# Experts' loop turned by three weight pieces, with an adding indirect transfer per block in place of stores and gathers

## The reference, cut to what matters

```
logits = h @ router_w + router_b            # 512 x 32
top, ids = top_k(logits, 4); gate = softmax(top)
for each token t and each of its 4 experts e:
    up   = h[t] @ w1[e] + b1[e]             # 1024 -> 2 x 1024, a gate part and a linear part
    hid  = silu-like(min(gatepart, 7)) * (clip(linear, -7, 7) + 1)
    y[t] += gate[t, e] * (hid @ w2[e] + b2[e])
x = x + mod * y                             # then a last RMS norm is the output
```

## Time and profile before

| | us |
|---|---|
| median of 3 runs | 3776.75 (3775.6 to 3782.47) |
| the profiled execution | 3776.74 |
| its span, first to last instruction | 3774.8 |
| mean granted TensorE clock | 0.923 of 2.4 GHz |
| busy in the span: TensorE, VectorE, ScalarE, GpSimd | 3347.7, 2305.7, 1548.4, 117.1 |
| experts' loop, first weight matmul to last | 2488.2 to 3705.9 |
| combining, its first DMA to the last addition to the residual | 3717.3 to 3758.2 |

### The profile page before, as it was taken

The page is one execution under the profiler, slowest core; times in us unless marked ns, Lnnn a source line. Parts: engine busy times, 40 slices in busy tenths (PEclk is TensorE's granted clock), DMA queues, the critical chain, the costliest instruction groups (busy, mean ns, idle before and its releaser), DMA issues. The chain is left out here.

```text
span 3774.8 us, 47052 instructions
## 1 busy us (share of the span) xinstructions
PE 3347.7 (89%) x16502; PEld 2588.1 (69%) x16503; DVE 2305.7 (61%) x2926; ACT 1548.4 (41%) x1933; POOL 117.1 (3%) x113
## 2 busy tenths in 40 slices
PE   7887998999968878899987878879999999999996
PEld 5655886884446567788756655667777777777774
DVE  4375665347422454455444474478888888888885
ACT  1262332010033621100123153357777777777772
POOL 0000000000000000000000000000000000000001
PEclk8888999999979987799988989879999999999996
DMA  5401222232102000122273101279999999999995
GB/s 160 154 24 45 89 100 80 99 89 89 67 27 64 1 1 1 50 100 92 89 290 120 56 9 34 77 313 399 363 357 359 361 352 359 364 355 360 359 346 216
DMA packets 182773, 648.58 MB, mean 172 GB/s; under 512 B 14033, under 2 KB 95825, under 8 KB 126210
## 3 DMA queue, kind: packets, MB, share of 16 engines
q1 hardware_dynamic: 165474, 600.56, 43.6%
q0 software_dynamic: 7056, 25.69, 1.8%
q10 hardware_dynamic: 10128, 20.76, 1.4%
HBM read 612.83 MB, written 36.75 MB: 172 GB/s over the span
## 5 line engine op out<-in xcount | busy, mean ns | idle before, releaser
L488 DVE TENSOR_TENSOR experts_rest<-experts_weights,experts_leading 128x2048 fp32r<-128x2048 f32 x384 | 875.3, 2286 | 109.7 <-ACT experts_leading L2990 109.7
L2990 ACT CAST experts_leading<-experts_weights 128x2048 fp32r<-128x2048 f32 x384 | 716.9, 1907 | 50.7 <-ACT experts_y L2982 22.2
L494 PE MATMUL psum<-experts_leading,experts_xT_leading 128*128 128x512 f32 x1024 | 410.9, 401 | 51.5 <-DVE experts_rest L488 51.5
L496 PE MATMUL psum<-experts_leading,experts_xT_rest 128*128 128x512 f32 x1024 | 406.2, 397 | 0.0
L495 PE MATMUL psum<-experts_rest,experts_xT_leading 128*128 128x512 f32 x1024 | 405.6, 396 | 0.0
L494 PEld LDWEIGHTS psum<-experts_leading,experts_xT_leading 128*128 128x128 f32 x1024 | 194.7, 190 | 107.4 <-DVE experts_rest L488 65.3
L496 PEld LDWEIGHTS psum<-experts_leading,experts_xT_rest 128*128 128x128 f32 x1024 | 194.6, 190 | 46.8
L495 PEld LDWEIGHTS psum<-experts_rest,experts_xT_leading 128*128 128x128 f32 x1024 | 194.6, 190 | 43.8
L494 PE MATMUL psum<-experts_leading,experts_hidden_leading 128*128 128x512 f32 x512 | 210.3, 411 | 0.0
L496 PE MATMUL psum<-experts_leading,experts_hidden_rest 128*128 128x512 f32 x512 | 201.2, 393 | 0.0
L495 PE MATMUL psum<-experts_rest,experts_hidden_leading 128*128 128x512 f32 x512 | 201.1, 393 | 0.0
(11 more groups left out here) (757 smaller groups left out, 6802.4 us busy)
## 6 DMA issues: line engine op xcount, KB each, us to landing
experts_weights<-in_w_up SPq DMA_DIRECT2D x256, 1024.0 KB, 6.8
experts_weights<-in_w_down SPq DMA_DIRECT2D x128, 1024.0 KB, 7.5
ada_unit<-in_w_ada SPq DMA_DIRECT2D x12, 2048.0 KB, 17.7
expert_rows<-experts_y ACTq DMA_DIRECT2D x66, 256.0 KB, 7.2
merge_first<-in_w_merge SPq DMA_DIRECT2D x16, 768.0 KB, 4.4
merge_weights<-in_w_merge SPq DMA_DIRECT2D x16, 768.0 KB, 4.1
ff_up_first<-in_w_up SPq DMA_DIRECT2D x11, 1024.0 KB, 4.8
ff_up_weights<-in_w_up SPq DMA_DIRECT2D x11, 1024.0 KB, 4.7
```

The source lines that it names most:

```text
L488: return dve.tensor_tensor(out, src, leading.bitcast(F32), ALU.subtract)
L494: pe.matmul(out, lh, rh, start=start, stop=False)
L496: return pe.matmul(out, ll, rh, start=False, stop=stop)
L2990: act.copy(leading[h % LEADING], place(ring, h)).then_inc(masked, 1)
```

## The change

It has four parts.

1. *The loop is turned by three halves* (`AHEAD = 3`). SP loads halves 0 to 2 of block 0 already in `route`, as soon as `block_expert` is known (which is computed earlier there), into a ring at the top of the memory that both stages share (`ExpertWeights`). ScalarE masks halves 0, 1 and 2 of block b+1 inside the body of block b: 0 between mask_hidden(2) and (3), 1 behind mask_hidden(3), 2 behind keep_y(0). VectorE splits half 0 of b+1 between split(11) and split_hidden(3), and half 1 behind split_x. SP's body loads 3 to 11 of block b, then 0 to 2 of b+1. The experts of unfilled blocks are read as at most 31, and all engines bound their loop by the number of filled blocks instead of reading each block's expert.
2. *y is scaled and added in DRAM.* `keep_y` copies the two halves of y inside the same block, scaled by the lane's gate (`gate_slots`), and GpSimd adds them to `expert_sums` with one indirect DMA of 128 rows (`compute_op=ALU.add`), and waits for it to land before it gathers again. Unfilled lanes add to rows past the 512. The rows are zeroed first, with five stores from SP ahead of the loop; the zero stores of unfilled blocks go.
3. *Routing* makes two more tables: `gate_of[lane, block]` (16 more products of `in_lane` with `in_block` times gate, behind those of `row_of` on TensorE) and `target_of`. `dest` goes.
4. *Combining* loads 4 groups of sums with plain DMAs from SP, directly behind b2's, and the residual behind them. The 16 gathers and VectorE's 16 steps go.

```diff
 # route
             @block.sync
+                sp.wait_ge(known, 1)
+                first = sp.value_load(block_expert[0:1, 0:1], min_val=0, max_val=EXPERTS - 1)
+                for h in range(AHEAD):
+                    weights.load(k, sp, first, h, weights.landed[h])
             @block.scalar
-                act.wait_ge(blocked, 1)
+                act.wait_ge(blocked, 2)
             @block.tensor
+                pe.wait_ge(passed_, 1)
+                pe.matmul(k.psum[0:1, 5 * BANK:5 * BANK + B], k.c("one")[0:E, :], past[:, :], start=True, stop=True)
...
                 last.then_inc(placed, 1)
                 pe.wait_ge(spreaded, TT)
+                pe.wait_ge(gated_blocks, 1)
+                for t in range(TT):
+                    for n in range(K):
+                        last = pe.matmul(k.bank(1, B), in_lane[:, t, n, :], in_block[:, t, n, :],
+                                         start=(t == 0 and n == 0), stop=(t == TT - 1 and n == K - 1))
+                last.then_inc(gates_placed, 1)
             @block.vector
+                dve.wait_ge(weighted, TT)
+                dve.tensor_tensor(in_block[:, :, :, :].rearrange("p t k b -> p (t k) b"),
+                                  in_block[:, :, :, :].rearrange("p t k b -> p (t k) b"),
+                                  gate[:, :, :].rearrange("p t k -> p (t k)").unsqueeze(2).broadcast_to([P, TT * K, B]),
+                                  ALU.mult).then_inc(gated_blocks, 1)
...
+                dve.wait_ge(gates_placed, 1)
+                v.then(dve.tensor_copy(gate_of[:, :], k.bank(1, B)))

 # experts
+            filled = eng.value_load(block_expert[0:1, SLOTS_MAX + 2:SLOTS_MAX + 3], min_val=1, max_val=SLOTS_MAX + 1)
             with eng.Fori(0, (SLOTS_MAX + 1) // 2) as i:
+                with eng.If(2 * i < filled):
+                    body(i, 0, 2 * i)
+                    with eng.If(2 * i + 1 < filled):
+                        body(i, 1, 2 * i + 1)
             @block.sync
+                def body(i, s, b):
+                    mine, following = expert_at(b), expert_at(b + 1)
+                    for h in range(AHEAD, HALVES):
+                        sp.wait_ge(consumed, b * HALVES + h + 1)
+                        weights.load(k, sp, mine, h, landed[h])
+                    for h in range(AHEAD):
+                        sp.wait_ge(consumed, (b + 1) * HALVES + h + 1)
+                        weights.load(k, sp, following, h, landed[h])
+                        if h == 0:
+                            load_bias(1 - s, following)
+                load_bias(0, expert_at(0))
+                for t in range(TT + 1):
+                    sp.dma_start(sums[t * P:(t + 1) * P, :].rearrange("p (a n) -> p a n", n=HALF),
                                  zero[:, :].unsqueeze(1).broadcast_to([P, D // HALF, HALF])).then_inc(zeroed, 16)
+                blocks(sp, body)
             @block.gpsimd
+                def body(i, s, b):
+                    gather(1 - s, i + s, b + 1)
+                    pool.tensor_copy(targets[:, s:s + 1], target_of[:, bass.ds(b, 1)]).then_inc(targeted, 1)
+                    pool.tensor_copy(gate_slots[:, s:s + 1], gate_of[:, bass.ds(b, 1)]).then_inc(gates_kept[s], 1)
+                    wait_apart(pool, targeted, b + 1, passed)
+                    for u in range(2):
+                        wait_apart(pool, y_copied[u], b + 2, passed)
+                    pool.indirect_dma_start(out=sums, out_offset=bass.IndirectOffsetOnAxis(ap=targets[:, s:s + 1], axis=0),
+                                            in_=y[:, :, :].rearrange("p u n -> p (u n)"), in_offset=None, compute_op=ALU.add
+                                            ).then_inc(added, 16)
+                    wait_apart(pool, added, b * 16 + 16, passed)
+                pool.wait_ge(zeroed, 16 * (TT + 1))
             @block.scalar
+                    def keep_y(u):
+                        act.wait_ge(consumed, (b + 1) * HALVES + HALVES - 1 + u)
+                        act.wait_ge(gates_kept[s], i + 1)
+                        act.activation(y[:, u, :], k.bank(2 + u), ACT.Copy, scale=gate_slots[:, s:s + 1]).then_inc(y_copied[u], 1)
-                    mask(0)
-                    mask(1)
-                    store(0, b)
-                    mask(2)
-                    store(1, b)
-                    mask(3)
+                    mask(3, b)
...
                     keep_x(1 - s, i + s)
                     mask(11, b)
                     mask_hidden(2)
+                    mask(0, b + 1)
                     mask_hidden(3)
+                    mask(1, b + 1)
+                    keep_y(0)
+                    act.wait_ge(bias_landed[1 - s], (i + s) * 16 + 16)
+                    mask(2, b + 1)
+                    keep_y(1)
             @block.vector
-                    for h in range(4):
-                        split_half(h)
+                    split_half(2, b)
+                    split_half(3, b)
...
                     split_hidden(2)
                     split_half(11, b)
+                    split_half(0, b + 1)
                     split_hidden(3)
                     split_x(1 - s, i + s)
+                    split_half(1, b + 1)

 # combine
                 sp.dma_start(b2[:, :], k.dram["b2_3"]).then_inc(landed, 16)
-                sp.wait_ge(gathered[N // 2 - 2], 16)
+                for t in range(TT):
+                    sp.dma_start(acc[:, t, :], sums[t * P:(t + 1) * P, :]).then_inc(loaded[t], 16)
                 sp.dma_start(k.x[:, :, :].rearrange("p k t -> p (k t)"), residual).then_inc(back, 16)
-            @block.gpsimd
-                for n in range(N):
-                    t, c = n // TOP_K, n % TOP_K
-                    pool.indirect_dma_start(out=got[:, n, :], out_offset=None, in_=results,
...
             @block.vector
-                    dve.wait_ge(gathered[n], 16)
...
             @block.tensor
-                    pe.wait_ge(weighed, TOP_K * (t + 1))
+                    pe.wait_ge(loaded[t], 16)
```

More of the change, by code:

```diff
@@ L2779, in _, with __init__, half, load @@
                 dve.tensor_scalar(row_of[:, 0:B], k.psum[:, 6 * BANK:6 * BANK + B], float(T), None, ALU.add).then_inc(kept, 1)
[L2780 to L2783 removed]
+                v.do(dve.tensor_scalar(apart[:, :], k.psum[:, 6 * BANK:6 * BANK + B], 0.0, k.c("lanes_on")[:, 0:1], ALU.is_equal,
+                                       ALU.mult))
+                v.then(dve.scalar_tensor_tensor(target_of[:, :], k.psum[:, 6 * BANK:6 * BANK + B], float(T), apart[:, :], ALU.add,
+                                                ALU.add))
+                dve.wait_ge(gates_placed, 1)
+                v.then(dve.tensor_copy(gate_of[:, :], k.bank(1, B)))
                 dve.wait_ge(gated, 1)
                 v.then(dve.tensor_copy(gate_by_expert[:, :], k.psum[0:E, 7 * BANK:7 * BANK + T]))
[L2789 to L2793 removed]
+class ExpertWeights:
+    def __init__(self, k):
+        size = 6 * 2 * (KD // 2 * BANK)
+        self.ring = k.high("experts_weights", [P, 6, size // 6])
+        self.at = k.places[-1]
+        self.landed = [k.nc.alloc_semaphore(f"experts_first{n}_landed", num=160 + n) for n in range(AHEAD)]
+    def half(self, h):
+        wide = KD // 2 * BANK
+        u, part = (h // 2, h % 2) if h < 8 else (4 + (h - 8) % 2, (h - 8) // 2)
+        return self.ring[:, u, part * wide:(part + 1) * wide]
+    def load(self, k, sp, expert, h, landed):
+        wide = KD // 2 * BANK
+        u, part = (h // 2, h % 2) if h < 8 else ((h - 8) % 2, (h - 8) // 2)
+        src = k.dram["w_up_3" if h < 8 else "w_down_3"][bass.ds(expert, 1), u, :, part * wide:(part + 1) * wide]
+        sp.dma_start(self.half(h), src.rearrange("a p n -> p (a n)")).then_inc(landed, 16)
+def experts(k, rows, row_of, block_expert, bias_parts, sums, x_rows, index, first_gathered, weights, gate_of, target_of):
+    nc = k.nc
+    UNITS, HALVES, LEADING = 4, 12, 4
     HALF, WIDE = 2 * P, KD // 2 * BANK
@@ L2797, in experts @@
     with k.stage("experts") as (sb, sem):
-        ring = sb("weights", [P, LOADS, 2 * WIDE])
-        rest = k.over("experts_rest", ring[:, :, :], [P, LOADS, 2 * WIDE])
+        rest = k.over("experts_rest", weights.ring[:, :, :], [P, 6, 2 * WIDE])
         places = [k.over(f"experts_leading{n}", x[:, :, :], [P, 2, WIDE]) for n, x in enumerate((k.h, k.x))]
@@ L2972, in _, with mask @@
             def _(act):
+                def mask(h, b):
+                    act.wait_ge(landed[h], b * 16 + 16)
+                    act.wait_ge(consumed, b * HALVES + h + HALVES - LEADING + 1)
+                    act.copy(leading[h % LEADING], weights.half(h)).then_inc(masked, 1)
                 def keep_x(s, i):
@@ L3040, in split_x, with body @@
                               x_t.leading[:, s, :, :].rearrange("p k n -> p (k n)")).then_inc(x_split[s], 1)
-                def body(i, s, b, e):
-                    def split_half(h):
-                        dve.wait_ge(masked, b * HALVES + h + 1)
```

(2 more changed lines are left out.)

211 lines of the change are left out of this document (86 added, 125 removed).

## The result

The change makes the kernel slower: 3866.65 us (median of 4 runs, 3862.05 to 3870.88) against 3778.98 us for the kernel before in the same session (3775.6 to 3782.47), a ratio of 1.0231 with a 95% interval of 1.0216 to 1.0246. The profiled execution's span is 3862.5 us, 87.7 more than before's.

The account below looks back on a forecast made before the run. The loop was taken as bound by TensorE plus seams. From 3776.74 us: -51.9 (seams) -8.0 (clock) +3.2 (split_hidden(3) delay) +0 (stores) +3 (backlog) -2.3 (start) +0 (end) -8.0 (combining) = -64.0, so 3713 us; range 3697 to 3730.

Parts of the forecast that it names:

- The seams: Between two blocks, where TensorE wastes 0.89 or 2.51 us: all 31 seams close, 51.9 us off.
- The clock: Slow TensorE clock spells behind long seams in five blocks: gone with the holes, 8.0 us off, 0 as other bound.
- third rival: The ring sets the block's length: slower than before once L exceeds 14.1, 3800 or 3837 us; chance 0.14.
- the ring: GpSimd's cycle per block of adding transfer, landing, gather, landing, turning and down products; 24 + L us long.
- Stores, gathers and the adding transfer: GpSimd's queue in the loop: the gather behind the adding transfer's landing still comes in time; no stall, 0 us.
- L: The adding transfer's time to its landing in the loop: taken at 10.4 us, bounds 7.2 and 16.8.
- The break-even: In the loop, L of 14.1 us, above which the ring costs more than all gains, 64 us over 31 blocks.
- rival 2: DMA engines bound the loop at 359 GB/s, so only start and combining gain: 3766 us; chance 0.06.
- The start: Routing to first matmul: first matmul near 2483.7 against 2488.22, half 3 2.2 us late; net 2.3 us off.
- the backlog: First blocks, where loads land late during the first fill: 3 us on (0 to 10).
- The end: Last matmul to the combining's first DMA: about 11.5 us against 11.4, taken at 0 (+-4).
- The combining: Final stage without its 16 gathers and VectorE steps: 32.9 us against 40.9, 8.0 us off.

Follow-up runs that it names:

- the late wait: The changed kernel with GpSimd's wait for the adding transfer's landing moved behind the next gather; 3717.6 us, ratio 0.9841 to the kernel before.
- the plain scatter: The changed kernel with the indirect transfer writing its rows in place of adding them, waits as they are; 3778.78 us in one run.
- Zeroing in the routing: The kernel with the late wait, its five zero stores of the sums moved from the loop's head into the routing; 3715.54 us, ratio 0.9827.
- y is copied early: The changed kernel with ScalarE's keep_y(1) ahead of mask(2) of the next block instead of behind it; 3814.17 us, ratio 1.0103.

## Why the prediction was wrong, step by step

- **The seams** (-51.9): right. (The figures in brackets are the prediction's terms.) No seam in the loop is late by more than 0.4 us after, and with the late wait a block takes 36.28 us, where 36.2 was predicted. The 0.1 us for split_hidden(3) came as waits of about 0.2 at every second block.
- **The clock** (-8.0): right only where the holes go. With the late wait the clock is 1.00 in the loop. In the kernel after, the new holes bring slow spells instead of removing them, and by the last leg (14.13 against 12.73 with the late wait) they cost 1.4 us of the 4.8 by which a block is too long; the prediction's third rival counted the ring without them. The turning behind the 2.69 us hole above took 1.97 us against the 1.03 of the earlier trace rows. The stretches of that block ahead of the hole, behind it and a little later, with the columns of the earlier trace rows:

```profile
3120.00:3127.00 7.00, 7.00 (x34) 5.75 (x33) 6.38 (x7) 5.10 (x6) 3.34 (x4) 1.00 1.01 424
3130.00:3133.00 3.00, 2.79 (x11) 2.60 (x12) 0.51 (x2) 0.79 (x1) 0.00 (x0) 0.53 1.03 426
3134.00:3140.00 6.00, 6.00 (x29) 4.82 (x28) 3.65 (x3) 3.21 (x3) 0.00 (x0) 1.00 0.57 191
```

- **Stores, gathers and the adding transfer** (0): this is the step that failed. The ring was seen, its order was right, and the sentence "So there is no stall while L stays under 12.0" was wrong. By that sentence the measured landing of 12.3 would have cost 0.3 us a block, and the hole at the turning measures 3.1. The legs without L were put at 24.0 us and measure 28.0; L (to the copy behind it, as it acts) was put at 10.4 and measures 13.0. The legs had 1.7 us of slack (34.4 against 36.1) and were 6.6 short. In the table every leg came out longer than it was put, and the traces show in part by what. The first: y is ready 1.9 us behind the seam (put at 1.6), and GpSimd issues 0.85 behind that (put at 0.1), as at the seam of 3144.50:

```profile
3145.70 0.69 ACT L3048 ACTIVATE experts_y<-psum,experts_gate_slots 128x512 f32<-128x512 f32 x1
...
3147.26 2.34 POOL L2939 DMA_INDIRECT expert_sums<-experts_y,experts_targets  x1 [23.13 <-ACT experts_y L3048]
```

What GpSimd does between the landing and the gather's issue was put at 1.3 us without a row that shows it behind a DMA's landing, and takes 2.4 (12.96 and 1.71, less the 12.3 to the landing). The gather's 8.4 became 9.4: the 11 gathers whose issuing instruction took 1.0 us landed after 8.7, the 11 with 2.5 after 10.1 (before, 8.3 with 1.0 and 8.5 with 2.9); they go out into a burst of 424 GB/s (the first of the stretches above), which is argued as a cause and not shown. The last leg was put at full clock. The loop took 1313.4 us, where the prediction's terms give 1166.2 (1217.7 less 51.9 and 8.0, and 3.2, 3 and 2.2 for half 3 on top). These 147.2, the 7.9 at the end and the combining's 3.5 less than put are the 151.6 us by which the profiled execution (3864.38) missed 3712.7.
- **The break-even** of rival (3), 14.1, was the same mistake: with 28.0 it is near 10 (36.1 + 2.1 - 28.0), and the plain scatter, 3779 us with a landing of 10.1, lies on it. The rival named the mechanism and the sign, and with its threshold computed from the undersized legs it seemed to need a long L; it had a chance of 0.14. That its time came out on the right side (3800 to 3837, for an L of 14.8 to 16) is in part luck: at the measured 12.3 its own formula gives no loss at all.
- **The rule of the Trainium skill** (Collectives: The Full Stack, "The bandwidth ceiling: the fold count and why AG ≠ RS ≠ AR"), half a copy's rate for an add, agrees with the engines' time of q0 (2.63 us against 1.31 for a gather and 1.28 for a plain scatter). The estimate of 14.8 that I made of it does not: the landing measured 12.3. I had doubled 6.4 us of the gather; the stretch from the first packet to the last is 4.6 us for the plain scatter and 6.1 for the add, so it does not double with the engines' time.
- **The DMA engines as the bound** (rival 2): wrong. 376 GB/s over 900 us, and 424 and 426 in the short stretches above. The Trainium skill, HBM Reference, "Specifications (TRN2)", says that a core alone gets above its 358, and the runs agree.
- **The start** (-2.3) and the backlog (+3): the first weight matmul came at 2483.8, where 2483.7 was predicted. That is in part luck: counted from the first instruction of the routing stage it came 48.0 us behind instead of 51.8 before, 3.8 less where 4.5 was put, and that first instruction itself comes at 2433 to 2448 in the eight profiled executions, with the same code ahead of it. Half 3 was ready later than put (a wait of 4.76 instead of 2.2): SP issued it at 2488.45 instead of 2487, behind the five zero stores. Zeroing in the routing removes this. The gather of the kernel before had 24 to 30 us to spare ahead of the turning, not "over 30"; nothing hung on it.
- **The end** (0): 7.9 us were lost. The wait for the landing in front of 8 empty turns was in the text and its price was not. **The combining** (-8.0): -11.5. Its 64 turnings took 9.34 us in one piece, at a granted clock of 0.79 in the mean (3833 to 3842), where I had carried 0.50 over from the earlier trace rows.

## What to carry to other kernels

When a wait is put into an in-order queue, add up the whole ring that it closes, every leg with the time it takes under the new load, and ask for a margin over the sum of a size with the unknowns: here 1.7 us of slack stood against five legs of which one had never been measured. Then look for the place in the queue where nothing urgent stands behind the wait. The transfer needed only to be over before the next transfer of its kind, not before the gather, and moving the wait across the gather turned a 2.3% loss into a gain of 1.6%.

## What the runs showed of the hardware

- An adding indirect transfer of 128 rows of 4 KB lands 12.3 us after its issue in the kernel after and 10.9 where y is copied early, beside weight loads; DMA moves 333 to 376 GB/s in all in these kernels. A plain scatter of the same rows takes 10.1, a gather 8.4 in the median in the kernel before, 9.4 after and 10.9 with the late wait. The last transfer of the loop, with nothing beside it, took 6.0 as an add and 3.3 as a plain scatter.
- The add occupies the 16 DMA engines for 2.63 us, a plain scatter for 1.28 and a gather for 1.31, for the same bytes.
- An adding transfer keeps GpSimd 2.3 us for its issue in the kernel after (74.8 us for 32) and 1.6 where y is copied early (51.2 for 32); a gather keeps it from 1.0 to 2.9.
- TensorE's clock fell to its 1.2 GHz level behind 20 of 22 holes of 2.6 to 3.8 us in the kernel after, behind 12 of 23 of 1.6 to 4.8 with y copied early, and behind 7 of 23 of 0.6 to 3.5 with the plain scatter. The length of the hole alone does not decide it: two of 2.7 and 2.8 us in the kernel after left the clock full, and one of 1.9 with the plain scatter did not.
